# A two-layer hybrid decoder step on one core: narrow matmuls widened with zero rows, and expert weights moved in 1 MB halves

## The reference

```
for layer in range(2):
    if layer == 0: mix = ab_mixer(x)      # GLA (4 heads, 128x256 states) and Mamba-2 SSD (16 heads), w_in, w_out
    else:          mix = hgrn_mixer(x)    # 8 heads, 128x128 states, w_in, w_out
    x = layer_norm(ALPHA * x + mix)
    x = layer_norm(ALPHA * x + moe(x))    # 16 experts of width 512, top 2 of one group of 4

def moe(t):
    gates = top-2 weights of the router
    for e in range(16):
        he = silu(t @ w_gate[e]) * (t @ w_up[e])      # 1024 -> 512
        y += gates[:, e:e + 1] * (he @ w_down[e])     # 512 -> 1024
```

## Time and profile before

| | us |
|---|---|
| median of 3 runs (lowest to highest) | 1199.57 (1198.38 to 1200.24) |
| the profiled execution's own time | 1198.36 |
| its span in the trace | 1196.6 |
| PE busy | 1121.0 (94%) |
| DVE, ACT, POOL busy | 393.5, 226.1, 90.4 |
| experts of layer 0, first gate product to last scatter | 423.6 to 651 |
| experts of layer 1 | 953 to 1179 |
| HGRN heads (first output block to last) | about 728 to 874 |
| bytes read from HBM, of which expert matrices | 268 MB, 201 MB |

### The profile page before, as it was taken

The page is one execution under the profiler, slowest core; times in us unless marked ns, Lnnn a source line. Parts: engine busy times, 40 slices in busy tenths (PEclk is TensorE's granted clock), DMA queues, the critical chain, the costliest instruction groups (busy, mean ns, idle before and its releaser), DMA issues.

```text
span 1196.6 us, 13356 instructions
## 1 busy us (share of the span) xinstructions
PE 1121.0 (94%) x5467; PEld 727.2 (61%) x5467; DVE 393.5 (33%) x965; ACT 226.1 (19%) x438; POOL 90.4 (8%) x129
## 2 busy tenths in 40 slices
PE   7999999799999699999998899999998699999996
PEld 4877777566687545353534787777777535354543
DVE  1346554544411521111113235453322501112124
ACT  2312111113211210000001243332312110000002
POOL 1111110221100200000000000000121100000000
PEclk9999999899999599999999899997988699999998
DMA  8722221552393159999999331122267089999991
GB/s 336 282 76 75 76 75 71 214 211 79 119 377 146 72 236 429 414 427 427 427 428 427 123 143 45 67 73 73 75 243 319 1 367 412 429 428 428 427 387 37
DMA packets 21824, 284.21 MB, mean 238 GB/s; under 512 B 2648, under 2 KB 4056, under 8 KB 4728
## 3 DMA queue, kind: packets, MB, share of 16 engines
q1 hardware_dynamic: 19728, 268.51, 54.6%
q0 software_dynamic: 1536, 14.32, 2.9%
q10 hardware_dynamic: 496, 0.47, 0.2%
HBM read 267.99 MB, written 15.40 MB: 237 GB/s over the span
## 4 chain that ended last, share of the span: by engine, by line
PE 88%; DVE 5%; DMA 4%; ACT 2%; issue 1%; POOL 0%; ACTq 0%; DVEq 0%; POOLq 0%
PE bank L1095 17%; PE bank L678 13%; PE bank L1118 8%; PE bank L1251 7%; PE bank L990 5%; PE bank L1081 4%; PE bank L1130 4%; PE bank L1238 4%; DMA ring<-in_w_up 3%; PE bank L756 3%; PE bank L772 2%; PE bank L774 2%; PE bank L1042 1%; PE bank L911 1%; PE bank L743 1%; PE bank L1016 1%
## 5 line engine op out<-in xcount | busy, mean ns | idle before, releaser
L1095 PE MATMUL bank<-ring,A 128*64 128x512 f32 x880 | 224.9, 597 | 4.1 <-DMA ring<-in_w_up 2.4
L678 PE MATMUL bank<-xT,ring 128*128 128x264 f32 x704 | 174.9, 395 | 0.0
L678 PEld LDWEIGHTS bank<-xT,ring 128*128 128x128 f32 x704 | 128.2, 190 | 43.8 <-issue 25.5
L1095 PEld LDWEIGHTS bank<-ring,A 128*64 128x64 f32 x880 | 75.0, 138 | 126.5 <-issue 126.3
L1118 PE MATMUL bank<-ring,W 128*64 128x512 f32 x448 | 113.4, 595 | 0.9 <-ACT W L1532 0.9
L1251 PE MATMUL bank<-xT,ring 128*128 128x264 f32 x320 | 92.0, 419 | 2.8 <-ACT A L1576 2.8
L2074 DVE TENSOR_TENSOR W<-W,bank 128x512 f32<-128x512 f32 x16 | 11.0, 687 | 209.8 <-PE bank L1095 209.8
L1118 PEld LDWEIGHTS bank<-ring,W 128*64 128x64 f32 x448 | 35.0, 137 | 60.9 <-issue 59.8
L1251 PEld LDWEIGHTS bank<-xT,ring 128*128 128x128 f32 x320 | 58.8, 199 | 16.8 <-issue 6.9
L1095 PE MATMUL bank<-A 128*64 128x512 f32 x144 | 63.3, 592 | 2.5 <-DMA ring<-in_w_up 2.5
L1130 PE MATMUL bank<-W,A 128*128 128x264 f32 x256 | 63.5, 393 | 1.7 <-ACT A L1527 1.7
(11 more groups left out here) (294 smaller groups left out, 1274.1 us busy)
## 6 DMA issues: line engine op xcount, KB each, us to landing
ring<-in_w_gate SPq DMA_DIRECT2D x28, 2048.0 KB, 14.3
ring<-in_w_down SPq DMA_DIRECT2D x28, 2048.0 KB, 16.2
ring<-in_w_up SPq DMA_DIRECT2D x27, 2048.0 KB, 17.5
ring<-in_w_ab SPq DMA_DIRECT2D x11, 2048.0 KB, 7.5
ring<-in_w_c SPq DMA_DIRECT2D x8, 2048.0 KB, 12.2
A<-in_w_up SPq DMA_DIRECT2D x5, 2048.0 KB, 16.5
ring<-in_w_oab SPq DMA_DIRECT2D x4, 2048.0 KB, 10.3
A<-in_w_gate SPq DMA_DIRECT2D x4, 2048.0 KB, 14.5
```

The source lines that it names most:

```text
L678: mm = pe.matmul(ab_bank(m)[:, 0:T], slot(AB_IN0 + m // 4, 8)[:, c, (m % 4) * P:(m % 4 + 1) * P], xT[:, c, :], start=(c == 0), stop=(c == ...
L1095: mm = pe.matmul(bank[i][64 * j:64 * j + 64, :], xg[:, 2 * (pair % 2) + j, c, :], slot(n0 + 6 * pair + 2 * i + j, 8)[:, c, :], start=(c == ...
```

## The change

1. **Halves.** Each expert matrix is moved as two transfers of 1 MB (`fill_half`). For gate and up a half is four of the eight contraction chunks; for down the host lays the matrix out anew so that a half holds the 512 output columns that go to one bank. The order on SP within a pair is, for each of gate, up, down: first half of expert 0, first half of expert 1, second half of expert 0, second half of expert 1. PE waits for halves (`half_ready`) and raises `moe_gate`, `moe_up` and `moe_down` after each half; SP refills the first half of a place once the first half was read. ACT copies bank 4 after the first half of down.
2. **Zero rows.** The updates in the heads take 64 rows (partitions 64 to 127), those in SSD and the two spreads 128 rows. The rows without data are cleared to zero by POOL: `dtT` (now 128 partitions) before `consts_made`, the head areas once before GLA and once before HGRN, `s_xdec` and `s_bmask` after stage 1. DVE waits for `rows_cleared` before it writes the 8 rows.
3. Pairs of semaphores that are used one after the other share one name.

```diff
+            def fill_half(n, half, src):
+                if n in EXTRA_FREE:
+                    name, value = EXTRA_FREE[n]
+                    sp.wait_ge(sem(name), value)
+                elif BEFORE[n] >= 0:
+                    name, value = last_reader(BEFORE[n])
+                    sp.wait_ge(sem(name), value - 1 + half if name in MOE_READ else value)
+                sp.dma_start(place_of(n)[:, HALF_W * half:HALF_W * (half + 1)], src[:, HALF_W * half:HALF_W * (half + 1)]
+                             ).then_inc(sem(f"{FILLED[half]}{PLACE[n]}"), 16)
...
-                    for i in range(6):
-                        fill(n0 + 6 * pair + i, views[i % 2][i // 2])
+                    for i in range(3):
+                        for half in range(2):
+                            for j in range(2):
+                                fill_half(n0 + 6 * pair + 2 * i + j, half, views[j][i])
...
+            names["vdec_rows"] = area(b + 1536, 256)[DR:P, :]
+            names["kmask_rows"] = area(b + 2048, NB, P)[DR:P, :, :]
...
-        dtT = sb("dtT", [16, 3, T])
+        dtT_rows = sb("dtT", [P, 3, T])
+        dtT = dtT_rows[0:16]
...
+            st.add(pool.memset(dtT_rows[:, :, :], 0.0))
+            st.settle()
             pool.sem_inc(sem("consts_made"), 1)
+
+            def clear_rows():
+
+                for h in range(2):
+                    hb = head_area(h)
+                    st.add(pool.memset(hb["vdec_rows"], 0.0))
+                    st.add(pool.memset(hb["kmask_rows"], 0.0))
+                st.settle()
+                pool.sem_inc(sem("rows_cleared"), 1)
+
+            clear_rows()
...
             stage_end(pool, 1)
+            st.add(pool.memset(s_xdec[:, :], 0.0))
+            st.add(pool.memset(s_bmask[:, :, :], 0.0))
+            st.settle()
+            pool.sem_inc(sem("rows_cleared"), 1)
             store_states(GLA_ST0, 4, gla_s, "gla_stored")
...
             stage_end(pool, 4)
+            clear_rows()
...
-                            mm = pe.matmul(dec_update(b, dv), hb["kmask"][:, b, :], hb["vdec"][:, 0:dv],
+                            mm = pe.matmul(dec_update(b, dv), hb["kmask_rows"][:, b, :], hb["vdec_rows"][:, 0:dv],
...
-                                       ident[0:16, h:h + 1].to_broadcast([16, P]), dtT[:, 1, 0:NP],
+                                       ident[:, h:h + 1].to_broadcast([P, P]), dtT_rows[:, 1, 0:NP],
...
-                        pe.matmul(bank[7 - 2 * (b % 2)][:, :], s_bmask[0:NB, b, :], s_xdec[0:NB, :], start=True, stop=True
+                        pe.matmul(bank[7 - 2 * (b % 2)][:, :], s_bmask[:, b, :], s_xdec[:, :], start=True, stop=True
...
-                        for j in range(2):
-                            slot_ready(pe, n0 + 6 * pair + 2 * i + j)
                         for c in range(DC):
+                            if c % 4 == 0:
+                                for j in range(2):
+                                    half_ready(pe, n0 + 6 * pair + 2 * i + j, c // 4)
...
-                        mm.then_inc(sem(MOE_READ[i]), 1)
+                            if c % 4 == 3:
+                                mm.then_inc(sem(MOE_READ[i]), 1)
...
-                    for j in range(2):
-                        slot_ready(pe, n0 + 6 * pair + 4 + j)
                     pe.wait_ge(sem("hT_copied"), p + 1)
                     for i in range(2):
+                        for j in range(2):
+                            half_ready(pe, n0 + 6 * pair + 4 + j, i)
...
-                                               slot(n0 + 6 * pair + 4 + j, 4)[:, f, 512 * i:512 * (i + 1)],
+                                               slot(n0 + 6 * pair + 4 + j, 8)[:, 4 * i + f, :],
...
-                    mm.then_inc(sem("moe_down"), 1)
+                        mm.then_inc(sem("moe_down"), 1)
...
-                    act.wait_ge(sem("moe_down"), p + 1)
+                    act.wait_ge(sem("moe_down"), 2 * p + 1)
...
+                    dve.wait_ge(sem("rows_cleared"), 3 if layer else 1)
                     st.add(dve.tensor_copy(hb["vdec"][:, 0:dv], bank[2][DR:DR + NB, P:P + dv]))
...
-        return w.reshape(layers, n, rows // P, P, c).transpose(0, 1, 3, 2, 4).reshape(layers, n, P, -1)
+        return w.reshape(layers, n, rows // P, P, c // 512, 512).transpose(0, 1, 3, 4, 2, 5).reshape(layers, n, P, -1)
```

More of the change, by code:

```diff
@@ L191, in trunk_program @@
         NTH = [PLACE[:n + 1].count(PLACE[n]) for n in range(len(PLACE))]
+        HALF_W = SLOT_W // 2
+        IN_MOE = [MOE0 <= n < C_IN0 or n >= MOE1 for n in range(len(PLACE))]
+        NTH_HALF = [sum(IN_MOE[m] and PLACE[m] == PLACE[n] for m in range(n + 1)) for n in range(len(PLACE))]
+        FILLED = ("first_filled", "slot_filled")
         BEFORE = [max([m for m in range(n) if PLACE[m] == PLACE[n]], default=-1) for n in range(len(PLACE))]
@@ L290, in last_reader @@
                     pair, i = divmod(n - MOE0, 6)
-                    return MOE_READ[i // 2], pair + 1
+                    return MOE_READ[i // 2], 2 * (pair + 1)
                 if n < HG_ST0:
@@ L300, in last_reader @@
                 pair, i = divmod(n - MOE1, 6)
-                return MOE_READ[i // 2], PAIRS + pair + 1
+                return MOE_READ[i // 2], 2 * (PAIRS + pair + 1)
             def fill(n, src):
@@ L324, in fill_over @@
                     for name in MOE_READ:
-                        sp.wait_ge(sem(name), PAIRS * (layer + 1))
+                        sp.wait_ge(sem(name), 2 * PAIRS * (layer + 1))
                     with sp.Fori(0, E_N) as e:
@@ L456, in spread_bank, with half_ready @@
             return bank[(5, 1, 2, 1)[pr]]
+        def half_ready(eng, n, half):
+            eng.wait_ge(sem(f"{FILLED[half]}{PLACE[n]}"), 16 * (NTH[n] if half else NTH_HALF[n]))
         def slot_ready(eng, n):
@@ L1174, in experts @@
                 with pe.If(flag > 0):
-                    pe.wait_ge(sem("over_gates"), layer + 1)
+                    pe.wait_ge(sem("over_gates"), 3 * layer + 1)
                     for b in range(2):
                         tr = pe.transpose(bank[7][0:16, b * P:(b + 1) * P], rt[:, 6, b, :], ident[:, :])
-                    tr.then_inc(sem("over_turned"), 1)
+                    tr.then_inc(sem("over_gates"), 1)
                     with pe.Fori(0, E_N) as e:
                         x = E0 + e
-                        pe.wait_ge(sem("over_sel"), x + 1)
-                        pe.wait_ge(sem("over_gates_copied"), layer + 1)
-                        pe.matmul(bank[6][:, 0:NP], osel, ogT, start=True, stop=True).then_inc(sem("over_spread"), 1)
+                        pe.wait_ge(sem("over_sel"), 3 * x + 1)
+                        pe.wait_ge(sem("over_gates"), 3 * layer + 3)
+                        pe.matmul(bank[6][:, 0:NP], osel, ogT, start=True, stop=True).then_inc(sem("over_sel"), 1)
                         for i in range(2):
@@ L1208, in experts @@
                     with pe.If(flag < 1):
-                        for name, k in (("turned", 1), ("spread", E_N), ("gu", 4 * E_N), ("down", DC * E_N), ("read", E_N),
+                        for name, k in (("gates", 1), ("sel", E_N), ("gu", 4 * E_N), ("down", DC * E_N), ("read", E_N),
                                         ("resummed", 1)):
@@ L1301, in bound_tanh @@
             def bound_tanh():
-                act.wait_ge(sem("lb_diff"), 1)
-                act.activation(lbc[:, 0, :], lbc[:, 2, :], ACT.Tanh, scale=0.5).then_inc(sem("lb_tanh"), 1)
+                act.wait_ge(sem("lb_steps"), 1)
+                act.activation(lbc[:, 0, :], lbc[:, 2, :], ACT.Tanh, scale=0.5).then_inc(sem("lb_steps"), 1)
             def gate_logs(out, z, n):
@@ L1313, in dt_exp @@
             def dt_exp():
-                act.wait_ge(sem("dt_scanned"), 1)
-                act.activation(dtT[:, 2, :], dtT[:, 1, :], ACT.Exp).then_inc(sem("dt_ready"), 1)
+                act.wait_ge(sem("dt_steps"), 1)
+                act.activation(dtT[:, 2, :], dtT[:, 1, :], ACT.Exp).then_inc(sem("dt_steps"), 1)
             def take_ab(m):
@@ L1548, in experts @@
                         x = E0 + e
-                        act.wait_ge(sem("over_spread"), x + 1)
+                        act.wait_ge(sem("over_sel"), 3 * x + 2)
                         act.wait_ge(sem("over_hidden"), 4 * x + 2)
-                        act.copy(ogb, bank[6][:, 0:NP]).then_inc(sem("over_spread_copied"), 1)
+                        act.copy(ogb, bank[6][:, 0:NP]).then_inc(sem("over_sel"), 1)
                         for f in range(4):
@@ L1567, in forget_logs @@
             def forget_logs():
-                act.wait_ge(sem("hg_forget"), 1)
-                act.activation(A[:, 8:16, :], A[:, 8:16, :], ACT.Ln).then_inc(sem("hg_log"), 1)
+                act.wait_ge(sem("hg_steps"), 1)
+                act.activation(A[:, 8:16, :], A[:, 8:16, :], ACT.Ln).then_inc(sem("hg_steps"), 1)
             def take_c(m):
@@ L1841, in _ @@
```

(5 more changed lines are left out.)

56 lines of the change are left out of this document (28 added, 28 removed).

## The result

| | before | after |
|---|---|---|
| median, us (lowest to highest, runs) | 1199.62 (1196.05 to 1200.43, 6) | 1178.64 (1175.57 to 1193.06, 6) |
| ratio to before, 95% interval | | 0.985 (0.980 to 0.990) |
| the profiled execution, and its span | 1198.36, 1196.6 | 1175.57, 1173.7 |
| PE busy | 1121.0 | 1101.1 |

What follows compares the result with a forecast made beforehand. PE was taken to bound the kernel, with 88% of the span. The profiled 1198.36 less 7.0 us for the two expert stops, and 0 for zero rows, gave 1191.4; the median was put at 1193.0, range 1185.5 to 1199.0.

Steps and rivals of the forecast that it cites:

- A: Whole kernel: the forecast itself, 1190 to 1196 us with its bounds; chance 0.56.
- part 1: Last expert pair of each layer: half transfers remove PE's stops before up, 4.4 and 2.9 us, together 7.0 after rests.
- The price of the packets: Expert stream: smaller rows and more transfers cost 0 to 1.8%, 0 to 3.4 us; 2 us taken.
- The first refill: Start of the expert stage: the stream restarts at 427.2 and not 430.67, 3.4 us earlier; net 1 us.
- The clears: POOL clearing rows: 0.9 us for `dtT`, 2.9 for head areas, 1.7 for `s_xdec` and `s_bmask`, all covered.
- D: Expert stages: 1 MB transfers slow the stream; the old stops return, or at 5% the kernel takes 1211 us; chance 0.08.
- E: Expert stages: second halves set the pair anyway, only layer 0's clock is won, 1.9 us: 1197.7; chance 0.03.
- so a wider contraction is free: PE products: 8 rows by 512 columns take 636 ns, 128 rows 645, so more rows cost nothing.
- Cost 0: POOL's clears of the zero rows: nothing added; 1.7 us if all of their cover were gone.
- part 2: Zero rows in head and SSD products: a gain could only come from the clock; taken as 0.
- B: HGRN heads: the slow head vanishes too, by zero rows or earlier timing, 6.5 us: 1186.5; chance 0.20.
- C: HGRN heads: a second head falls to half clock, 6.5 us more: 1199.5, no change; chance 0.13.

Runs made afterwards that it cites:

- e1: The changed kernel with all narrow products back at 8 and 16 rows, so halves only: 1191.36 us, ratio 0.993 to the kernel before.
- e5: The changed kernel as it is, measured again in five rounds: 1181.65 us, ratio 0.987 to the kernel before.
- e2: The changed kernel with whole 2 MB transfers, zero rows kept: 1193.54 us, ratio 0.993 to the kernel before.
- e3: The changed kernel with 32 rows instead of 128 in the SSD updates and spreads: 1191.34 us, ratio 0.992 to the kernel before.
- e7: The changed kernel, but SP refills either half of a place only when the whole matrix was read: 1189.39 us, one run.
- e4: The changed kernel with 8 rows back in the GLA and HGRN head updates, SSD left at 128: 1184.99 us, ratio 0.988 to the kernel before.
- e10: The kernel before, with 64-row outputs ahead of 128-row ones and the next head's first decode update behind its state update: 1190.71 us, ratio 0.994.
- e8: The changed kernel, with 64-row outputs ahead of 128-row ones and the next head's first decode update behind its state update: 1163.92 us, ratio 0.971.

## Why the prediction failed

**Right.** A, the forecast for part 1. Halves alone brought 7.1 us against 7.0, with an interval of 5 to 12, and in the changed kernel's profile 4.0 in layer 0 against 4.4 and 2.2 in layer 1 against 2.9, where 0.33 us of stop was left. The price of the packets, put between 0 and 1.8% and taken as about 1.05%, was 1.1%. The first refill came 3.7 us into gate, where 3.4 was reckoned. The clears took a little less than they were priced at (0.76 us for `dtT` against 0.9), and nobody on the chain waits for them. D is out, since the stream runs at 420 GB/s, and E, since the stops are gone.

**Wrong: "so a wider contraction is free", with "Cost 0" and "I take 0 from part 2".** This is the step that failed: the term of part 2 was put at nothing and was worth about 8.5 us. The step compared the mean durations of products of 8 and of 128 rows, 636 and 645 ns, and took their likeness for the price of the edit. Two things were wrong in it. The 128-row group was a bad yardstick: four instructions at one place, which take 644 ns after the change too, while the widened updates now take 592.

```profile
L951 PE MATMUL bank<-W 128*128 128x512 f32 x32 | 16.3, 592 | 0.0
...
L991 PE MATMUL bank<-W 128*128 128x512 f32 x4 | 2.3, 644 | 0.0
```

And a duration isn't the cost. What a product costs on PE is the distance from its start to the next start, and that holds the next weight load when it isn't covered: 0.19 us at each of the update's two edges, 0.38 in all, of which the mean durations show 0.09 (44 ns on each of two instructions). The section on the profile before says that the spacing tells more than the duration; the step didn't use it. The timeline of PEld, with 0.34 and 0.76 us of "issue" before loads, would have shown it. By the aligned starts the term was worth 7.8 to 8.1 us in SSD (e1 and before, each against e5) and 0.5 in GLA, and it is why the range was missed: 1193.0 - 8.5 = 1184.5, which lies below the range, 3 us above e5 and 6 above the first measurement. What is left is within the spread of one kernel's runs; part of the first measurement's 21 us is luck.

**Wrong for its reason: B.** The slow head did vanish from the profile, 6.5 us in it, but not by the zero rows, and it isn't lost for good: e2, e3 and e7 have such heads with 64 rows, and e4 and e10 have none with 8. "Only one of eight equal heads falls, so it is marginal" was right, and should have led to the statement that it comes and goes between runs of one kernel. The profile's gain of 22.8 us holds this 6.5; the medians' gain doesn't hold it, unless such heads are rarer on average after the change, which the profiles can't tell. **C** is the same thing with the other sign, and no rival to a median either.

A rule of the Trainium skill that spoke for a gain, the one on tiling modes named above, was not weighed. The Trainium skill, "TensorE: Matmul & The Clock Gate", section "LDWEIGHTS (loading the stationary operand)", states that a load takes as long for 32 rows as for 128. The trace agrees for the load's own length, 0.18 us for 8 rows and 0.19 for 128 in the single loads of SSD. That says nothing of when a load may start, and this is what the zero rows changed.

## What to carry to other kernels

Price an edit of PE's products by the spacing of starts in the timeline of PE and PEld, never by the mean duration of a group; a load that starts with its product, and "issue" before it, is a load in the open. Keep products with equal numbers of rows next to one another, or fill a narrow one with zeros to its neighbours' rows: here each change of rows cost 0.14 to 0.19 us, and zero rows and order together were worth 29 us of 1200 (e8's 35.9 less the 7.1 of the halves); order alone, with unequal rows, 8.6. By the traces the same holds for the columns of the weights, transpositions apart; nobody has tried here what ordering by columns would bring. Where a stream and its reader run nearly level, split both the wait and the give-back; each alone left the stop.

## What the runs showed that was not expected

- A change in the number of rows between neighbouring products (8, 16 or 32 against 128; 64 against 128; 8 against 64) keeps the next weights from being loaded under the running product: 0.19 us a change in SSD, 0.14 in the output blocks. At 128 rows, the same is seen in the traces at every change between 128 and 64 columns, about 0.1 us, but not where the 64 columns belong to a transposition.
- Two 64-row products on partitions 0 to 63 and 64 to 127 run together: starts 0.01 us apart, sixteen instructions in 1.64 us for 2.17.
- The clock falls to 0.50 for stretches of 3 to 14 us in which PE is busy throughout, in GLA, in SSD and in HGRN. In HGRN PE had no idle time ahead of them either; in SSD it had waited 0.86 us. They lie at other places from one profile to the next. What starts a fall stays open.
- Rows of 8 KB for 16 KB and transfers of 1 MB for 2 MB slow a full stream by 1.1%.
